# Forget attention of a decoder layer: exp over pairs of PSUM banks, with a look-ahead counted in groups

## The reference

```python
q, k = rmsnorm(q, g_qB), rmsnorm(k, g_kB)          # per head
s = q @ k.T * HEAD_DIM ** -0.5 + c[q_pos] - c[k_pos]
s = where(key_pos <= q_pos, s, -inf)               # causal
p = softmax(s)
out = p @ v
```

## Time and profile before

| | us |
|---|---|
| Time, median of 2 runs | 3595.29 (3593.06 to 3597.53) |
| The profiled execution, its own time | 3595.43 |
| Its span on the slowest core (core 7) | 3593.8 |
| Span of the fastest core (core 5) | 3572.0 |
| PE busy | 2959.2 (82%) |
| ACT busy | 1563.2 (43%) |
| DVE busy | 1396.2 (39%) |
| POOL busy | 767.2 (21%) |

### The profile page before, as it was taken

One profiled execution on the slowest core, in us unless ns is written; L12 is line 12 of the kernel. 1 busy time (PEld: TensorE's weight loads), 2 busy tenths in 40 slices (PEclk: granted clock), 3 DMA queues, 4 the chain that ended last, 5 costly groups with the idle time before them and its releaser, 6 DMA issues.

```text
span 3593.8 us, 57936 instructions; the slowest of 8 cores (3572.0 to 3593.8 us)
## 1 busy us (share of the span) xinstructions
PE 2959.2 (82%) x15376; PEld 1350.2 (38%) x15376; DVE 1396.2 (39%) x2026; ACT 1563.2 (43%) x2951; POOL 767.2 (21%) x864
## 2 busy tenths in 40 slices
PE   2368776784688888988576599999999999999999
PEld 1134333442333434343232244444444444444444
DVE  4544665466755646545422131313131222313131
ACT  3335455544487786968666231312122131313131
POOL 0022222327777774000000110102020201011010
PEclk8588777875899999999889699999999999999999
DMA  4253334214665454000210455465655645554644
GB/s 115 89 164 106 101 100 127 85 60 135 160 170 161 149 175 134 8 6 8 69 33 24 134 149 211 141 196 159 189 192 169 213 148 181 171 188 146 213 139 146
DMA packets 268334, 472.83 MB, mean 132 GB/s; under 512 B 27616, under 2 KB 179552, under 8 KB 258656
## 3 DMA queue, kind: packets, MB, share of 16 engines
q1 hardware_dynamic: 240880, 385.73, 34.2%
q0 software_dynamic: 27136, 83.39, 8.0%
HBM read 404.81 MB, written 64.23 MB: 131 GB/s over the span
## 4 chain that ended last, share of the span: by engine, by line
PE 69%; ACT 9%; DVE 8%; DMA 6%; issue 5%; SPq 1%; POOL 0%; DVEq 0%; ACTq 0%; POOLq 0%
PE bank L233 69%; ACT arena L239 8%; DMA arena<-tabs 4%; DVE arena L242 3%; DVE arena L252 2%; SPq L62 1%; DVE arena L246 1%; DMA arena<-wsc_up 1%; DVE arena L256 1%; PE bank L236 1%; DVE arena L479 1%; DVE arena L259 1%; DMA stg<-w_in 1%; DMA stg<-w_mem_kv 1%; DMA arena<-wsc_gate 1%
## 5 line engine op out<-in xcount | busy, mean ns | idle before, releaser
L233 PE MATMUL bank<-arena 128*128 128x512 bf16 (+7 forms) x14492 | 2837.8, 353 | 376.1 <-DVE arena L242 115.3
L233 PEld LDWEIGHTS bank<-arena 128*128 128x128 bf16 (+3 forms) x14492 | 1273.1, 103 | 1907.8 <-issue 884.8
L239 ACT ACTIVATE arena<-bank 128x512 bf16<-128x512 f32 (+3 forms) x2202 | 1125.1, 631 | 967.6 <-PE bank L233 936.2
L242 POOL TENSOR_TENSOR arena<-arena 128x512 f32<-128x512 f32 (+1 forms) x224 | 337.7, 1508 | 2537.4 <-DVE arena L242 2293.7
L242 DVE TENSOR_TENSOR arena<-bank,arena 128x512 f32<-128x512 f32 (+2 forms) x576 | 420.1, 731 | 1065.0 <-PE bank L233 856.6
L239 ACT ACTIVATE arena<-arena 128x512 f32<-128x512 f32 (+4 forms) x464 | 282.9, 611 | 232.1 <-DVE arena L246 95.1
L242 DVE TENSOR_TENSOR arena<-arena 128x512 bf16<-128x512 bf16 (+3 forms) x384 | 211.5, 551 | 388.2 <-ACT arena L239 386.4
L239 ACT ACTIVATE arena<-bank,gcols 128x512 bf16<-128x512 f32 (+1 forms) x200 | 136.6, 687 | 328.0 <-PE bank L233 327.9
L252 DVE SCALAR_TENSOR_TENSOR arena<-bank,gcols,arena 128x512 bf16<-128x512 f32 (+2 forms) x260 | 194.0, 746 | 215.7 <-ACT arena L239 200.5
L242 DVE TENSOR_TENSOR arena<-arena,cb_sb 128x128 bf16<-128x128 bf16 (+1 forms) x448 | 153.3, 364 | 301.6 <-ACT arena L239 297.8
L256 DVE RECIPROCAL arena<-bank 64x512 f32<-64x512 f32 x64 | 215.0, 3359 | 74.1 <-PE bank L233 74.1
(11 more groups left out here) (23 smaller groups left out, 295.8 us busy)
## 6 DMA issues: line engine op xcount, KB each, us to landing
arena<-wsc_up SPq DMA_DIRECT2D x64, 1024.0 KB, 10.7
arena<-wsc_down SPq DMA_DIRECT2D x64, 1024.0 KB, 5.0
arena<-tabs SPq DMA_DIRECT2D x192, 256.0 KB, 2.9
arena<-wsc_gate SPq DMA_DIRECT2D x64, 768.0 KB, 5.1
arena<-wsc_br SPq DMA_DIRECT2D x64, 320.0 KB, 4.7
stg<-w_in SPq DMA_DIRECT2D x34, 512.0 KB, 6.1
arena<-x SPq DMA_DIRECT2D x64, 256.0 KB, 4.3
jst<-w_up POOLq DMA_DIRECT2D x64, 256.0 KB, 3.3
```

The source lines that it names most:

```text
L233: P.op("pe", lambda e: e.matmul(out, lhsT=lhsT, rhs=rhs, start=start, stop=stop), reads, writes)
L239: P.op("act", lambda e: e.activation(out=out, in_=in_, func=func, **kw), reads, writes)
L242: P.op(eng, lambda e: e.tensor_tensor(out=out, in0=in0, in1=in1, op=op), reads, writes)
```

## The change

Full blocks of a group are taken in pairs. The eight PSUM banks become one tensor `psbig` of 4096 columns, of which `banks[i]` are slices, so that one exp can read two banks side by side (1024 columns) into one tile of 1024 columns. The six tiles become three (`PTp`), one for each pair of banks. The list of blocks becomes a list of groups of blocks: pairs for the full blocks, single ones for d0 to d3. A single one takes a whole pair of banks and a tile of 1024, and uses the first half. `LA` becomes 2, and counts these groups. Matmuls, masks, reciprocals and stores are the same in number and size; the dilated and the memory attention keep their exps of 512 columns.

```diff
-    banks = [st.enter_context(nc.psum_tensor("bank%d" % i, [128, 512], F32)) for i in range(8)]
+    psbig = st.enter_context(nc.psum_tensor("psbig", [128, 4096], F32))
+    banks = [psbig[:, i * 512:(i + 1) * 512] for i in range(8)]
...
-        NPT = 6
-        PT = [A.alloc(512) for _ in range(NPT)]
-        r_PT = [R() for _ in range(NPT)]
+        PTp = [A.alloc(1024) for _ in range(3)]
+        r_PTp = [R() for _ in range(3)]
...
-                blocks = []
+                groups = []
                 for tg in range(NTG):
-                    for kb in range(4 * tg + 4):
-                        blocks.append((tg, kb))
-                nblk = len(blocks)
+                    for kb in range(0, 4 * tg, 2):
+                        groups.append((tg, (kb, kb + 1)))
+                    for kb in range(4 * tg, 4 * tg + 4):
+                        groups.append((tg, (kb,)))
+                ngrp = len(groups)
...
+                def emit_S(gi):
+                    tg, kbs = groups[gi]
+                    p = gi % 3
+                    for s_, kb in enumerate(kbs):
...
+                        MM(banks[2 * p + s_][:, 0:n], Kt[0:70, kb * 128:(kb + 1) * 128], Qt[0:70, q0:q0 + n], True, True,
+                           [rK[kb // 4], rKa, rQ[tg], rQa], [rb[2 * p + s_]])
+                    if len(kbs) == 2:
+                        ACT(PTp[p][:, 0:1024], psbig[:, 2 * p * 512:2 * p * 512 + 1024], AF.Exp,
+                            [rb[2 * p], rb[2 * p + 1]], [r_PTp[p]])
+                    else:
+                        ACT(PTp[p][:, 0:n], banks[2 * p][:, 0:n], AF.Exp, [rb[2 * p]], [r_PTp[p]])
+                        TT("dve", PTp[p][:, 0:128], PTp[p][:, 0:128], mask4[:, 0:128], ALU.mult, [r_PTp[p], r_cb],
+                           [r_PTp[p]])
...
+                        MM(banks[ob][:, 128 * j:512], Vt[:, kb, hh, :], PTp[p][:, s_ * 512:s_ * 512 + n], kb == 0, last,
+                           [r_Vt[kb // 4], r_PTp[p]], [rb[ob]])
...
-                LA = 4
-                for bi in range(min(LA, nblk)):
-                    emit_S(bi)
-                for bi in range(nblk):
-                    if bi + LA < nblk:
-                        emit_S(bi + LA)
-                    emit_PV(bi)
+                LA = 2
+                for gi in range(min(LA, ngrp)):
+                    emit_S(gi)
+                for gi in range(ngrp):
+                    if gi + LA < ngrp:
+                        emit_S(gi + LA)
+                    emit_PV(gi)
```

More of the change, by code:

```diff
@@ L943, in phase_fox @@
                 Kt, rK, rKa = QK[kn_]
-                blocks = []
+                groups = []
                 for tg in range(NTG):
-                    for kb in range(4 * tg + 4):
-                        blocks.append((tg, kb))
-                nblk = len(blocks)
[L950 to L967, removed]
-                    ob = 6 + tg % 2
[L969 to L978, removed]
@@ new lines, in emit_S @@
+                def emit_S(gi):
+                    tg, kbs = groups[gi]
+                    p = gi % 3
+                    for s_, kb in enumerate(kbs):
+                        j = max(0, kb - 4 * tg)
+                        n = 512 - 128 * j
+                        q0 = tg * 512 + 128 * j
+                        MM(banks[2 * p + s_][:, 0:n], Kt[0:70, kb * 128:(kb + 1) * 128], Qt[0:70, q0:q0 + n], True, True,
[7 more added lines that the diff above has]
+                           [r_PTp[p]])
@@ new lines, in emit_PV @@
+                def emit_PV(gi):
+                    tg, kbs = groups[gi]
+                    p = gi % 3
+                    ob = 6 + tg % 2
+                    for s_, kb in enumerate(kbs):
+                        j = max(0, kb - 4 * tg)
+                        n = 512 - 128 * j
+                        last = (kb == 4 * tg + 3)
+                        MM(banks[ob][:, 128 * j:512], Vt[:, kb, hh, :], PTp[p][:, s_ * 512:s_ * 512 + n], kb == 0, last,
+                           [r_Vt[kb // 4], r_PTp[p]], [rb[ob]])
+                        if last:
+                            RECIP(rec[0:64, :], banks[ob][64:128, :], [rb[ob]], [r_rec])
+                            yb = yt[tg % 2]
+                            TT("dve", yb[0:64, :], banks[ob][0:64, :], rec[0:64, :], ALU.mult, [rb[ob], r_rec],
+                               [r_yt[tg % 2]])
+                            P.dma(ysc[256 + h * 64:256 + (h + 1) * 64, tg * 512:(tg + 1) * 512], yb[0:64, :],
+                                  reads=[r_yt[tg % 2]], writes=[ry(("b", h, tg))])
```

## The result

The changed kernel takes 3638 us, median of 7 runs, against 3597 for the kernel before beside it: ratio 1.0111, with a 95% interval of 1.0096 to 1.0127. That is 40 us, or 1.1%, slower. In some executions the cores of a die ran slower at a lower clock, whatever the kernel; the ratios leave those out, and where only such an execution was profiled, its cores 0 to 3, which did not, are read. The profiled execution took 3648.4 us, and its slowest core is core 2.

The account below looks back on a forecast made before the run. ACT was taken to pace the late groups, PE at half clock the heads' starts. Terms 16 + 10 + 3 + 6 = +35 on 3595.4 gave 3630 us; the case's own range was 3605 to 3660, the whole range 3592 to 3680.

Parts of the forecast that it names:

- Removed exps: Late groups 3 to 7, where ACT paces: 50 pairs a head save 0.064 us each, 3.2 us a head; ceiling 28.7 us.
- that rival: Full-block pairs: an exp over two banks costs two singles, so the 25 saved don't appear, 3655 us; chance 0.08.
- The stall at the diagonal: Diagonals of groups 3 to 7: ACT stands still 1.03 us each, 5.2 against 3.2 saved, +2.0 us a head, 16 in all.
- The first groups: Start of each head: 640 more PE columns between PV(d0) and PV(d3), 1.2 us a head, 10 in all.
- the clock, 6: Head starts: PE's longer wait may bring another half-clock piece of 3.4 us, 1.4 us a head; 0 to 11, taken as 6.
- The masks beside POOL: Heads 0 to 3, while POOL converts weights: slower masks, 371 ns against 222, now lie on the path, 3 us.
- The whole gain without the loss: Late groups: pairs pay and diagonals don't hurt, under 0.64 us of stall per diagonal, 3570 us; chance 0.12.
- the rival of 3686: Late diagonals: stalls drop PE's clock, a half-clock piece of 3.4 us at each, 56 us on top; chance 0.09.
- POOL's pace: Weight conversion on POOL: claimed to be paced by its own DMAs, listed under hidden or unchanged; no size given.

## Why the prediction was right

It said 3630 us, and a change of 35; it is 40 us, 1.1%. It gives two ranges, 3605 to 3660 and 3592 to 3680, and 3638 lies in both. By its own steps:

- **Removed exps.** 448 fewer, 0.064 saved each where ACT paces: the slope of the periods gives 0.915 for a pair against 0.916 forecast, and two exps in the new order cost 2.05 us a head, against 2.1 expected. An exp over two banks shows no price of its own; that rival falls.
- **The stall at the diagonal.** 1.03 us worked out, 1.04 measured, and in the same parts: with time 0 at the end of exp(d0), the exps of d2, d3 and the next pair were to end at 0.89, 1.34 and 2.79, and the medians over the 192 late diagonals of heads 4 to 7 on all cores are 0.89, 1.34 and 2.79. (Before, the order listing has one score of the next group ahead of PV(d0), not several as the text says; the sum does not use that.) Without the mask it is 0.7 as reckoned, and with the diagonal in pairs half of it goes. The periods of groups 4 to 6, forecast as 9.7, 11.5 and 13.3, are 9.69, 11.53 and 13.36. The sum for groups 3 to 7, from the means of heads 4 to 7, is 0.58 + 0.50 + 0.36 + 0.30 + 0.27 = 2.0 us a head, as forecast: 16 in all.
- **The first groups.** The mechanism held (the columns between PV(d0) and PV(d3) count at PE's clock), but the size was short. The terms for them were 10 us and, for the clock, 6. The means of heads 4 to 7 grew by 0.54, 1.07 and 1.00 in the three first periods. The first of these, from one head's last reciprocal to the next head's first, only the second head of a pair has, so it is 4 x 0.54 + 8 x 2.07 = 19 in all, for 16. The step that was off is "Three such groups per head, one of them at half clock": the period from group 0 to group 1 had 2.86 of its 6.49 us at half clock before and 6.05 of 7.56 after, the next 3.23 of 6.39 and 4.73 of 7.39. Time at half clock grew by 48 us a core, 6 a head, where I had taken half of one 3.4 us piece a head. By the prediction's own price (1.4 us for 3.4), the 19 us of it in heads 4 to 7 are some 8 us, an estimate, of the 9.4 by which their first periods grew. How the growth divides between the clock and the columns was not measured.
- **The masks beside POOL.** Forecast 3, measured 7. A mask in heads 0 to 3 took 467 ns on the slowest core after, where 371 before went into the sum; over the cores the means are 333 to 400 before and 426 to 463 after (in a slightly wider stretch), and 33 to 39 of the 128 masks took over 500 ns where 19 to 28 had. Why the same mask is longer was not tried. Not all of the 7 us need be masks: time at half clock in groups 3 to 7 of these heads grew from 1.1 to 4.2 us a head.
- **The rivals.** The whole gain without the loss (3570) needed under 0.64 us of stall, and there were 1.04. The clock did fall more, but at the heads' starts: in groups 3 to 7 of heads 4 to 7 no core has time at half clock, and in heads 0 to 3 it is the 4.2 us a head above, where the rival wanted 3.4 at each of five diagonals. So the rival of 3686 falls, with its true part in the terms above.
- **POOL's pace.** "Weight conversion on POOL is paced by its own DMAs" is not what the trace of before shows: in heads 0 to 3 of core 7 POOL is busy 281 of 372 us, and under 4 us of its waits end with a DMA. The sum does not use it.

The Trainium skill, Perfetto Trace Analysis, section Optimizing Scalar/DVE Operations, says that grouping operations can help where the engine is saturated, and that breaking them up may help where it is not but causes bubbles on other engines. The first rule agrees with the new order, where ACT was saturated in the late groups and fusing saved 15 us. The second does not decide this case as the prediction has it: the 58 us of the coarser order arise with single exps, so they are a matter of the order and not of the size of the instructions. In the old order single exps were 11 us better, though ACT was saturated in the late groups there too. The Trainium skill, ScalarE: Activation LUTs, section What ACT_TABLE_LOAD costs, gives an ACTIVATE with immediate scale and bias 186 ns fixed and an overlap of about 93 back to back, so by an estimate from it 93 ns are left; the runs give 64.

16 + 19 + 7 = 42 us against 43 of the phase. No term came out smaller than forecast, so the total is not right by errors that cancel. The rows show a granted clock of 0.50 behind the longer waits of PE; at which wait it falls was not tried.

## What to carry to other kernels

When instructions are fused, look at what the look-ahead counts: a depth of "two groups" is four blocks only while all groups are pairs, and where they are not, a handover that had cover comes on the path. Work out the chain there, engine by engine, before counting the fixed prices saved. A small operation on another engine in the middle of a chain (here a mask of 0.22 us, queued behind a reciprocal of 3.4) can be worth more than all the fixed prices; here, moving it to the engine with slack gave 59 to 64 us in the phase, where fused exps gave 17 to 22 even with the look-ahead mended.

## What was not expected of the hardware

- A mask of 128 columns on DVE takes 223 ns with POOL idle, and on the slowest cores 371 (before) and 467 (after) on average with POOL converting weights. In the changed kernel's first four heads the median is 226 ns and the longest 1754 (128-column masks of core 2), so the mean comes from a few that stand still.
- The clock counted for more than expected: taking the mask alone off DVE took the time at half clock from 82 us to 3 a core in the phase of the kernel before.
- One exp over two PSUM banks goes through its columns as fast as one over a single bank (0.490 us for 512): 0.915 us for 1024 columns back to back, mean record 1063 ns, in this view of the groups by form of core 2 (count, busy, mean ns), with the exps of d3 below it, before which ACT sat idle 52 us in all:

```profile
L239 ACT ACTIVATE arena<-psbig 128x1024 bf16<-128x1024 f32 x448 | 421.2, 1063 | 48.2 <-PE psbig L233 46.1 <-DVE arena L242 1.4
...
L239 ACT ACTIVATE arena<-psbig 128x128 bf16<-128x128 f32 x64 | 17.7, 277 | 52.2 <-PE psbig L233 49.9 <-DVE arena L242 2.0
```
